# The beginning of a decoder layer's mixer: keys from row pieces, turns of the normalised rows inside the value projection, and query banks emptied ahead of the next weight split

## Chip, cores and metric

The kernel runs on one core of a Trainium2 chip. The metric is device time in microseconds from the start of the program to its end; smaller is better. Engines are named as in the profile: PE is TensorE, PEld its weight loads, DVE is VectorE, ACT is ScalarE, POOL is GpSimd, SP is SyncE, which here only issues DMAs.

## What is computed

One decoder layer over 256 tokens of width 1024, all in fp32. The part that matters here is the beginning of the token mixer:

```
h = layer_norm(x, ln0_g, ln0_b)                     # 256 x 1024
proj = h @ w_in                                     # 256 x 6664
qkv, a, bt, z, xc, gb, gc, qm, gl = split(proj)
qkv = silu(causal_depthwise_conv(qkv, conv_qkv))    # 4 taps, 1536 channels
g = -(exp(a_log) * softplus(a + dt_bias))           # decay of each head
beta = sigmoid(bt)
...                                                 # gated delta rule, short conv
kv = mem @ w_mem_kv                                 # mem 256 x 1024
km, vm = split(kv, 2)                               # 512 key, 512 value columns
...                                                 # attention over mem, gates, w_o
x1 = layer_norm(alpha * h + mixer, ln1_g, ln1_b)
out = layer_norm(alpha * x1 + moe(x1), ln2_g, ln2_b)  # top 4 of 32 experts
```

The experts read all of `w_gate_up` and `w_down`: 32 experts of six 2 MB chunks each.

## The kernel before

**Products.** A 32-bit product in the mixer is made of three faster ones: each operand is split in a `hi` part (type fp32r) and a `lo` part, the rest, and PE adds hi x hi, hi x lo and lo x hi (function `three`, L1171 to L1173). So each weight has to be split before use: ACT casts to `w_hi` (L1048), then DVE or POOL subtracts to `w_lo` (L759). The table `LO_ENGINE` says which of the two does it for a piece.

**Weights.** SP brings mixer weights in slots of 2 MB (8 k-tiles of 128 rows x 512 columns), three raw slots in turn. A slot is split in four pieces of 128 x 1024 values; three split pieces can exist at a time (`SPLITS = 3`), so the split of piece q + 3 (a `prep` step) waits until piece q is used up. Slot 0 holds the key weights, slot 1 the value weights, slots 2 to 4 those of the twelve query, key and value units of the delta rule (`("qkv", 0)` to `("qkv", 11)`, called query units here), and so on to slot 20. Slot 0 comes in four DMAs by columns: each takes 128 of the 512 columns of all 1024 rows, which is 512 bytes in a row of HBM.

**Order.** `mixer_schedule` writes one list of steps, and each engine walks through this list in a loop, taking the steps that concern it. The list begins: turns of `mem` (`memT`, PE transposes into a bank, ACT and DVE split the result), four key units (`km`, each one piece, 24 matmuls of 256 columns), layer norm of the two token tiles (`ln`), the value projection (`vm`: two tiles, 48 matmuls of 512 columns, piece by piece, in `project_rows`), turns of the normalised rows (`hT`), the transposed convolution taps (`cols`), then query units, with the decay's small projection `ab` (24 matmuls of 256 columns against 8 weight columns) after the second of them, its transpose `abT` after the third, and `decay functions` (ACT) after the fourth. Later the steps of the delta rule (`g`) lie between units.

**Banks.** Units that fill a PSUM bank take banks 0 to 2 in turn (`bank_of`), so a unit waits until the unit three before it has been emptied. A query unit is emptied by DVE alone: one multiply for the first tap (L1632) and three multiply-adds (L1635); ACT then applies silu (L1027). A `prep` step stands ahead of the unit whose piece it waits for, so ACT casts and DVE subtracts the next piece before they touch that unit's bank.

**POOL.** Its list of mask constants (`masks`, `decay_masks`) stands ahead of all steps, and `level_masks` after `prep` 8.

**After the mixer.** The experts' chunks go into a ring of 12 slots. SP issues a chunk's DMA as soon as the slot's last content is used; the first three take the mixer's raw slots when the last weight pieces are split, and most of the others wait for the last matmul of `w_o` (L1215).

Of the kernel before, what the change touches and what calls it, by code (L numbers as in the profile page):

```python
# [33 lines left out]
ALU = mybir.AluOpType  # L34
# [3 lines left out]
P = 128  # L38
D = 1024
T = 256  # L40
NT = T // P
KD = D // P
H = 4
# [56 lines left out]
def mixer_schedule():  # L100
# [63 lines left out]
NOT_UNITS = ("decay functions", "g", "prep", "ln", "ya", "sum hi", "sum", "soft", "log decay", "cols", "ab split")  # L164
# [4 lines left out]
def hybrid_layer(nc, x, mem, ln0_g, ln0_b, w_in, conv_qkv, conv_mix, a_log, dt_bias, gdn_norm,  # L169
                 w_mem_kv, w_br, w_o, ln1_g, ln1_b, w_router, b_router, w_gate_up, b_gate_up,  # L170
                 w_down, b_down, ln2_g, ln2_b, out):
    with ExitStack() as ctx:
# [173 lines left out]
        piece_in = [sem(f"piece_in{n}") for n in range(4)]  # L346
# [17 lines left out]
        ab_split, ab_act, ab_dve = sem("ab_split"), sem("ab_act"), sem("ab_dve")  # L364
# [29 lines left out]
        piece_end, joint = {}, 0  # L394
        for u in UNITS:
# [11 lines left out]
        LO_ENGINE[0:12] = ["dve"] * 5 + ["pool"] * 4 + ["dve"] * 3  # L407
# [8 lines left out]
        def piece_views(q):  # L416
# [6 lines left out]
            elif MIXER_SLOTS[n] == ("kv", W) or kind == "wo":  # L423
# [73 lines left out]
        def pe_gdn(pe, name):  # L497
# [20 lines left out]
            elif name == "decay":  # L518

                pe.wait_ge(g_dve, GD["scalars"])  # L520
                for p in range(NPB):
                    mm(out4(p), spread(g_log, p // H, p % H), block_upper[:], start=True, stop=True)
# [239 lines left out]
        def slot_dma(sp, n, j=0):  # L762
# [10 lines left out]
            if n == 0:  # L773
                sp.dma_start(dst[:, :, j * P:(j + 1) * P], src[:, :, j * P:(j + 1) * P]).then_inc(piece_in[j], 16)
            else:
                sp.dma_start(dst, src).then_inc(raw_in[n % RAW], 16)

# [17 lines left out]
        MIXER_FILLS = [len(range(r or RAW, N_MIX, RAW)) if r < RAW else 0 for r in range(RING)]  # L795
# [30 lines left out]
        def _(sp):  # L826
            def bcast(dst, src, done):
                sp.dma_start(dst, src).then_inc(done, 16)

            slot_dma(sp, 0, 0)  # L830
            sp.dma_start(mem_tok, mem[0].rearrange("(t p) d -> p t d", p=P)).then_inc(mem_in, 16)
            for j in range(1, 4):
                slot_dma(sp, 0, j)
            slot_dma(sp, 1)
            sp.dma_start(hx[:], x[0].rearrange("(t p) d -> p t d", p=P)).then_inc(x_in, 16)
            bcast(lnp0[:, 0, :], ln0_g.rearrange("(a d) -> a d", a=1).broadcast_to([P, D]), lnp_in[0])
            bcast(lnp0[:, 1, :], ln0_b.rearrange("(a d) -> a d", a=1).broadcast_to([P, D]), lnp_in[0])
            rows = small_rows
# [80 lines left out]
        def _(pool):  # L919
# [16 lines left out]
            def masks():  # L936
# [3 lines left out]
                for n in range(LEVELS + 1):  # L940
# [950 lines left out]
```

## Time and profile before

| | |
|---|---|
| median of 3 runs | 1269.95 us (1269.81 to 1270.58) |
| the profiled execution: its own time | 1270.24 us |
| its span | 1268.5 us |
| PE busy | 1218.5 us, 96% |
| DVE busy | 400.8 us, 32% |
| ACT busy | 239.2 us, 19% |
| POOL busy | 141.1 us, 11% |
| DMA | 453.45 MB, mean 357 GB/s over the span |

The busy time of PE says little alone: an engine that runs slowly is also busy. The strip in 40 slices (31.7 us each) shows three stages. In the first slice PE is 80% busy and DMA over 90%; in slices 2 to 10 PE is over 90% busy and DMA between 10% and 70%; from slice 12 on both are over 90%, with 424 to 430 GB/s.

### The profile page before, as it was taken

To read this page: it belongs to the slowest core of one execution; us is meant where nothing else is said; L and a number is where in the kernel's file an instruction comes from. 1 tells how busy PE (TensorE), PEld (TensorE's weight loads), DVE (VectorE), ACT (ScalarE), POOL (GpSimd) and SP (SyncE) were. 2 spreads that over 40 slices of the span, in tenths; PEclk is the share of its full clock that TensorE was granted. 3 is DMA by queue.
4 is the path that set the end of the run, shared out by engine and by line. 5 is a ranking of instruction groups with operands and counts; after the bars stand their busy time and mean duration, and the time that the engine had idled before them with its cause. 6 is when DMAs were issued, how large, how long until landed. Compare 5 with 4: busy or idle time off the path is not lost.

```text
span 1268.5 us, 17229 instructions
## 1 busy us (share of the span) xinstructions
PE 1218.5 (96%) x7155; PEld 616.8 (49%) x7155; DVE 400.8 (32%) x787; ACT 239.2 (19%) x385; POOL 141.1 (11%) x105
## 2 busy tenths in 40 slices
PE   8799999999999999999999999999999999999995
PEld 7699999998843333333333333333333333333332
DVE  5685563534521221222222122122122222222114
ACT  4364344444310000010000000000000000000001
POOL 4433422455200000000000000000000000000000
PEclk9899999999999999999999999999999999999998
DMA  9533313595799999999999999999999999999995
GB/s 306 198 134 134 134 68 134 205 360 184 281 399 424 428 427 428 427 428 428 430 428 430 428 427 428 430 428 430 428 427 427 429 427 429 429 426 428 428 427 209
DMA packets 56412, 453.45 MB, mean 357 GB/s; under 512 B 6877, under 2 KB 11050, under 8 KB 31786
## 3 DMA queue, kind: packets, MB, share of 16 engines
q1 hardware_dynamic: 56362, 452.71, 86.3%
q8 instruction: 40, 0.66, 0.2%
q14 instruction: 10, 0.08, 0.0%
HBM read 451.64 MB, written 1.05 MB: 357 GB/s over the span
## 4 chain that ended last, share of the span: by engine, by line
PE 78%; DMA 9%; SPq 4%; DVE 4%; ACT 2%; issue 2%; POOL 0%; another core or an unknown queue 0%; DVEq 0%; ACTq 0%
PE bank L1357 30%; PE bank L1429 15%; DMA late<-in_w_gate_up_dram 8%; PE bank L1171 5%; PE bank L1172 5%; PE bank L1173 5%; PE bank L1328 4%; PE bank L1442 4%; SPq L792 4%; PE bank L1343 2%; PE bank L1417 2%; ACT late L1143 1%; DMA early<-in_ln_b_dram 1%; PE bank L1437 1%; DVE w_lo L759 1%
## 5 line engine op out<-in xcount | busy, mean ns | idle before, releaser
L1357 PE MATMUL bank<-late 128*64 128x512 f32 x1536 | 343.2, 595 | 5.1 <-DMA late<-in_w_gate_up_dram 5.1
L1429 PE MATMUL bank<-late 128*64 128x512 f32 x1024 | 230.1, 602 | 6.2 <-ACT late L1143 6.2
L1357 PEld LDWEIGHTS bank<-late 128*64 128x64 f32 x1536 | 106.7, 137 | 222.7 <-issue 209.8
L1429 PEld LDWEIGHTS bank<-late 128*64 128x64 f32 x1024 | 71.4, 138 | 142.9 <-issue 129.1
L1171 PE MATMUL bank<-act_hi,w_hi 128*128 128x256 f32 x448 | 129.4, 289 | 3.1 <-DVE early L1635 2.5
L1172 PE MATMUL bank<-act_lo,w_hi 128*128 128x256 f32 x448 | 125.8, 281 | 0.0
L1173 PE MATMUL bank<-act_hi,w_lo 128*128 128x256 f32 x448 | 125.8, 281 | 0.0
L1775 DVE TENSOR_SCALAR late<-bank 128x512 f32<-128x512 f32 x32 | 22.1, 692 | 308.2 <-PE bank L1357 308.2
L1357 PE MATMUL bank<-raw,late 128*64 128x512 f32 x512 | 116.7, 598 | 1.2 <-DMA raw<-in_w_gate_up_dram 1.2
L759 POOL TENSOR_TENSOR w_lo<-raw,w_hi 128x1024 fp32r<-128x1024 f32 x33 | 81.2, 2463 | 127.1 <-ACT w_hi L1048 127.1
L1171 PEld LDWEIGHTS bank<-act_hi,w_hi 128*128 128x128 f32 x448 | 84.3, 188 | 5.3 <-DVE early L1635 3.3
L1172 PEld LDWEIGHTS bank<-act_lo,w_hi 128*128 128x128 f32 x448 | 84.5, 189 | 0.1
L1173 PEld LDWEIGHTS bank<-act_hi,w_lo 128*128 128x128 f32 x448 | 84.4, 188 | 0.0
L1786 DVE COPY late<-bank 64x512 f32<-64x512 f32 x32 | 22.2, 694 | 191.3 <-PE bank L1429 191.3
L1136 ACT COPY late<-bank 128x512 f32<-128x512 f32 x33 | 19.3, 586 | 321.9 <-PE bank L1328 321.9
L1048 ACT CAST w_hi<-raw 128x1024 fp32r<-128x1024 f32 x56 | 58.5, 1046 | 90.2 <-issue 59.4
L1357 PEld LDWEIGHTS bank<-raw,late 128*64 128x64 f32 x512 | 34.0, 136 | 72.3 <-issue 69.0
L1442 PE MATMUL bank<-late 64*128 64x512 f32 x256 | 63.6, 615 | 1.0 <-DVE late L1846 1.0
L1145 ACT COPY late<-bank 64x512 f32<-64x512 f32 x32 | 18.5, 579 | 233.3 <-PE bank L1429 233.3
L1328 PE MATMUL bank<-hx,late 128*64 128x512 f32 x264 | 62.3, 592 | 0.0
L1141 ACT ACTIVATE late<-late 128x512 f32<-128x512 f32 x32 | 20.1, 629 | 179.7 <-DVE late L1775 179.7
L1790 DVE COPY late<-bank 128x256 f32<-128x256 f32 x31 | 13.2, 425 | 117.9 <-PE bank L1437 117.9
(319 smaller groups left out, 1194.4 us busy)
## 6 DMA issues: line engine op xcount, KB each, us to landing
late<-in_w_gate_up_dram SPq DMA_DIRECT2D x96, 2048.0 KB, 36.4
late<-in_w_down_dram SPq DMA_DIRECT2D x64, 2048.0 KB, 35.8
raw<-in_w_gate_up_dram SPq DMA_DIRECT2D x32, 2048.0 KB, 34.5
raw<-in_w_in_dram SPq DMA_DIRECT2D x8, 2048.0 KB, 8.7
early<-in_w_in_dram SPq DMA_DIRECT2D x6, 2048.0 KB, 8.4
raw<-in_w_br_dram SPq DMA_DIRECT2D x3, 2048.0 KB, 7.8
raw<-in_w_mem_kv_dram SPq DMA_DIRECT2D x4, 512.0 KB, 7.9
raw<-in_w_mem_kv_dram SPq DMA_DIRECT2D x1, 2048.0 KB, 10.9
```

The costliest lines, as they stand in the source:

```text
L759: ops.tensor_tensor(lo, src, as_f32(hi), ALU.subtract).then_inc(split_lo[who], 1)
L792: sp.dma_start(dst, src).then_inc(landed, 16)
L1048: a.copy(hi, src).then_inc(split_hi, 1)
L1171: mm(o, l_hi, r_hi, start=start, stop=False)
L1172: mm(o, l_hi, r_lo, start=False, stop=False)
L1173: return mm(o, l_lo, r_hi, start=False, stop=stop)
L1328: ins = mm(ps[0][64 * c:64 * c + 64, :], onehot[:, t, :], hx[:, t, 512 * c:512 * (c + 1)], start=(t == 0), stop=(t == NT - 1))
L1343: mm(ps[1 + n][64 * c:64 * c + 64, :], e_row[rows, :], bgu[rows, :], start=True, stop=False)
L1357: ins = mm(bk[64 * c:64 * c + 64, :], x_slotT[:, k % 4, 64 * (k // 4):64 * (k // 4) + 64], w[:, kk, at + 512 * c:at + 512 * (c + 1)], star ...
L1417: ins = tr(ps[3][:, c * P:(c + 1) * P], h_tok[:, c:4 * P:4], ident[:])
L1429: ins = mm(ps[3][64 * c:64 * c + 64, :], hidT[:, kk, 64 * q:64 * q + 64], w[:, kk, c * 512:(c + 1) * 512], start=(q == 0 and kk == 0), sto ...
L1442: ins = mm(ps[4 + 2 * t + c][:, :], scatter[64 * c:64 * c + 64, t * P:(t + 1) * P], y_tok[64 * c:64 * c + 64, :], start=False, stop=True, ...
```

## The change

Everything is in the first part of the mixer, and in the order around query units.

- SP asks for `mem` first, then two pieces of key weights, `x`, the other two, the layer norm's parameters, and then the value weights in four DMAs where there was one. Key and value pieces are cut by rows: two k-tiles of 128 rows, all 512 columns, so 2048 bytes in a row of HBM. The router's weights come after slot 5.
- With row pieces each key piece serves all four key units: `project_keys` keeps four banks (4 to 7) open and adds each piece's 24 matmuls to them. ACT copies all four at once afterwards (`km copy`).
- The turns of the normalised rows leave the banks in rotation; `turn_tile` makes them inside the value projection, before its third piece, in banks 4 to 7.
- The statistics of the layer norm are split from its application. `LO_ENGINE` has new entries for the first pieces.
- For query units the `prep` step now stands behind the unit. ACT does the first tap (a copy with a scale), and DVE the other three. The cast of the small decay weights and most of the decay's elementwise work go from DVE to ACT.
- POOL's mask constants are spread between its pieces.

```diff
...
-    order = [("prep", 0)] + [("memT", n) for n in range(4)] + [("prep", 1), ("prep", 2)]
-    order += [("km", n) for n in range(4)] + [("ln", 0, t) for t in range(NT)] + [("vm", n) for n in range(NT)]
-    order += [("hT", t, j) for j in range(2) for t in range(NT)] + [("prep", 9), ("cols",), ("prep", 10)]
-    order += [("qkv", 0), ("ab split",), ("qkv", 1), ("ab", 0), ("qkv", 2), ("abT", 0), ("qkv", 3), ("decay functions",)]
+    order = [("memT", 0), ("prep", 0), ("memT", 1), ("prep", 1), ("memT", 2), ("memT", 3)]
+    order += [("ln stats", t) for t in range(NT)] + [("prep", 2), ("prep", 3)] + [("ln root", t) for t in range(NT)]
+    order += [("km", 0), ("ln", 0, 0), ("prep", 4), ("prep", 5), ("ln", 0, 1), ("prep", 6), ("km copy",), ("prep", 7), ("prep", 8)]
+    order += [("hT", t, j) for t in range(NT) for j in range(2)] + [("prep", 9), ("vm", 0), ("prep", 10), ("vm", 1), ("cols",)]
+    order += [("ab split",)]
+    order += [("qkv", 0), ("qkv", 1), ("ab", 0), ("qkv", 2), ("abT", 0), ("qkv", 3), ("decay functions",)]
...
-        n = {"km": 1, "qkv": 1, "z": 1, "xc": 1, "gc": 1, "gb": 1, "qm": 1, "gate": 1}.get(s[0], 0)
+        n = {"qkv": 1, "z": 1, "xc": 1, "gc": 1, "gb": 1, "qm": 1, "gate": 1}.get(s[0], 0)
         if s[0] == "br":
             n = s[2] % 2
             uses[s] = [q]
-        if s[0] in ("vm", "wo"):
+        if s[0] in ("km", "vm", "wo"):
             n = 4 * (s[-1] == 0)
         if n:
             uses[s] = list(range(q, q + n))
-            out += [("prep", m + SPLITS) for m in uses[s] if m + SPLITS < 4 * N_MIX and ("prep", m + SPLITS) not in order]
+            preps = [("prep", m + SPLITS) for m in uses[s] if m + SPLITS < 4 * N_MIX and ("prep", m + SPLITS) not in order]
+            out += [s] + preps if s[0] == "qkv" else preps + [s]
             q += n
-        out.append(s)
+        else:
+            out.append(s)
...
+        for q in PIECES_OF["km", 0]:
+            joint += 1
+            piece_end[q] = (joint_piece, joint) if joint < 4 else (km_full, H)
+        joint = 3
...
-        LO_ENGINE[0:12] = ["dve"] * 5 + ["pool"] * 4 + ["dve"] * 3
+        LO_ENGINE[0:12] = ["dve", "pool", "dve", "pool"] + ["dve"] * 3 + ["pool"] * 2 + ["dve", "pool", "dve"]
...
-            if n == 0:
-                sp.dma_start(dst[:, :, j * P:(j + 1) * P], src[:, :, j * P:(j + 1) * P]).then_inc(piece_in[j], 16)
+            if kind == "kv":
+                sp.dma_start(dst[:, 2 * j:2 * j + 2, :], src[:, 2 * j:2 * j + 2, :]).then_inc(piece_in[4 * n + j], 16)
...
+            sp.dma_start(mem_tok, mem[0].rearrange("(t p) d -> p t d", p=P)).then_inc(mem_in, 16)
             slot_dma(sp, 0, 0)
-            sp.dma_start(mem_tok, mem[0].rearrange("(t p) d -> p t d", p=P)).then_inc(mem_in, 16)
-            for j in range(1, 4):
-                slot_dma(sp, 0, j)
-            slot_dma(sp, 1)
+            slot_dma(sp, 0, 1)
             sp.dma_start(hx[:], x[0].rearrange("(t p) d -> p t d", p=P)).then_inc(x_in, 16)
+            slot_dma(sp, 0, 2)
+            slot_dma(sp, 0, 3)
             bcast(lnp0[:, 0, :], ln0_g.rearrange("(a d) -> a d", a=1).broadcast_to([P, D]), lnp_in[0])
             bcast(lnp0[:, 1, :], ln0_b.rearrange("(a d) -> a d", a=1).broadcast_to([P, D]), lnp_in[0])
+            for j in range(4):
+                slot_dma(sp, 1, j)
...
-            sp.dma_start(wr[:], w_router[0].rearrange("(k p) e -> p k e", p=P)).then_inc(router_in, 16)
-            sp.dma_start(br_bc[:], b_router.broadcast_to([P, NE])).then_inc(router_in, 16)
             for n in range(3, N_MIX):
                 slot_dma(sp, n)
+                if n == 5:
+                    sp.dma_start(wr[:], w_router[0].rearrange("(k p) e -> p k e", p=P)).then_inc(router_in, 16)
+                    sp.dma_start(br_bc[:], b_router.broadcast_to([P, NE])).then_inc(router_in, 16)
...
+            before_mask()
+            block_masks(range(0, 4))
+            LEVEL_AFTER = {10: 0, 12: 1, 14: 2, 16: 3, 18: 4, 20: 5}
...
+                    if s[1] == 1:
+                        block_masks(range(4, LEVELS + 1))
+                    if s[1] == 3:
+                        decay_masks()
+                    if s[1] in LEVEL_AFTER:
+                        level_mask_of(LEVEL_AFTER[s[1]])
+                    if s[1] == 22:
+                        chunk_masks()
...
                 elif kind == "hT":
+                    act.wait_ge(h_turned, 2 * t + j + 1)
...
-                elif kind == "ln":
+                elif kind == "ln root":
+                    ln_root_of(0, s[1])
+                elif kind == "ln" and s[1] == 1:
                     ln_root_of(*s[1:])
-                elif kind == "km":
-                    a.copy(kmT[:, s[1], :], bank(s)).then_inc(free, 1)
+                elif kind == "km copy":
+                    for n in range(H):
+                        act.wait_ge(km_full, n + 1)
+                        a.copy(kmT[:, n, :], ps[4 + n][:, 0:T]).then_inc(km_copied, 1)
+                elif kind == "ab split":
+                    act.wait_ge(ab_in, 16)
+                    a.copy(w_ab_hi[:], w_ab).then_inc(ab_hi, 1)
...
                 elif kind == "qkv":
+                    if s[1] == 0:
+                        act.wait_ge(cols_ready, 1)
+                    act.wait_ge(bank_full[bank_of(s)], turn_of(s))
+                    a.activation(qkvT[:, s[1], :], bank(s), ACT.Copy,
+                                 scale=small_cols[:, 36 + s[1]:37 + s[1]]).then_inc(first_tap, 1)
                     if s[1] >= 1:
                         silu(s[1] - 1)
                     if s[1] == 11:
                         silu(11)
                 elif kind == "decay functions":
-                    act.wait_ge(ab_dve, 1)
-                    a.activation(ea, adt[:, 0, :], ACT.Exp)
-                    a.activation(beta, beta, ACT.Exp, scale=-1.0)
-                    step(a.activation(t_b, t_b, ACT.Exp))
-                    a.activation(t_b, t_b, ACT.Ln, bias=1.0).then_inc(ab_act, 2)
+                    act.wait_ge(bank_free[bank_of(("abT", 0))], turn_of(("abT", 0)))
+                    a.activation(t_c, pre_g, ACT.Relu)
+                    step(a.activation(t_b, pre_g, ACT.Abs))
+                    step(a.activation(ea, adt[:, 0, :], ACT.Exp))
+                    a.mul(ea, ea, -1.0)
+                    step(a.activation(beta, beta, ACT.Exp, scale=-1.0))
+                    a.activation(beta, beta, ACT.Identity, bias=1.0)
+                    step(a.activation(t_b, t_b, ACT.Exp, scale=-1.0))
+                    a.activation(t_b, t_b, ACT.Ln, bias=1.0).then_inc(ab_act, 1)
...
+            def project_keys():
+                for j in range(4):
+                    hi, lo = piece(PIECES_OF["km", 0][j])
+                    wait_copied(pe, "memT", j + 1)
+                    for n in range(H):
+                        for kk in range(2):
+                            k = 2 * j + kk
+                            ins = three(ps[4 + n][:, 0:T], hi[:, kk, n * P:(n + 1) * P], lo[:, kk, n * P:(n + 1) * P],
+                                        src_hi[:, k, :], src_lo[:, k, :], k == 0, k == KD - 1)
+                        if j == 3:
+                            ins.then_inc(km_full, 1)
+                    if j < 3:
+                        ins.then_inc(joint_piece, 1)
+            def turn_tile(t):
+                pe.wait_ge(ln_done, t + 1)
+                pe.wait_ge(km_copied, H)
+                for j in range(2):
+                    for k in range(4):
+                        ins = tr(ps[4 + 2 * t + j][:, k * P:(k + 1) * P], hx[:, t, (4 * j + k) * P:(4 * j + k + 1) * P], ident[:])
+                    ins.then_inc(h_turned, 1)
...
+                    if s == ("vm", 0) and j == 2:
+                        turn_tile(t)
...
-                    full()
                     o = qkvT[:, c, :]
-                    step(d.tensor_scalar(o, bk[:, 0:T], small_cols[:, 36 + c:37 + c], None, ALU.mult))
+                    v.wait_ge(first_tap, c + 1)
                     for back in range(1, 4):
...
-                    v.wait_ge(free, turn_of(s))
-                    step(d.tensor_scalar(t_a, pre_g, -1.0, None, ALU.mult))
-                    d.tensor_tensor(t_b, t_a, pre_g, ALU.min).then_inc(ab_dve, 1)
-                    step(d.tensor_scalar(t_c, pre_g, 0.0, None, ALU.max))
...
```

SP at the start of its list, before (`raw` is a weight slot; `early` is an area that holds `mem`, the layer norm's parameters and slot 2; `hx` holds `x`):

```order
L774 DMA raw<-in_w_mem_kv_dram 128x8x128
L831 DMA early<-in_mem_dram 128x2x1024
L774 DMA raw<-in_w_mem_kv_dram 128x8x128 x3
L776 DMA raw<-in_w_mem_kv_dram 128x8x512
L835 DMA hx<-in_x_dram 128x2x1024
L828 DMA early<-in_ln_g_dram 128x1024
L828 DMA early<-in_ln_b_dram 128x1024
L839 DMA small_rows<-in_conv_qkv_dram 48x128
```

and after:

```order
L847 DMA early<-in_mem_dram 128x2x1024
L787 DMA raw<-in_w_mem_kv_dram 128x2x512 x2
L850 DMA hx<-in_x_dram 128x2x1024
L787 DMA raw<-in_w_mem_kv_dram 128x2x512 x2
L845 DMA early<-in_ln_g_dram 128x1024
L845 DMA early<-in_ln_b_dram 128x1024
L787 DMA raw<-in_w_mem_kv_dram 128x2x512 x4
L858 DMA small_rows<-in_conv_qkv_dram 48x128
```

`mem` has moved ahead of the first key piece and `x` between the key pieces; the one value DMA stood ahead of `x` and is now four behind the parameters. A key piece was 128x8x128 and is 128x2x512.

ACT between query units 2 and 4, before (L1048 casts a weight piece, L1027 is silu, L1068 to L1071 are the decay functions):

```order
L1048 CAST w_hi<-raw 128x1024
L1027 ACTIVATE early<-early 128x256
L1048 CAST w_hi<-raw 128x1024
L1027 ACTIVATE early<-early 128x256
L1068 ACT_TABLE_LOAD
L1068 ACTIVATE tiny<-adt 128x4
L1069 ACTIVATE tiny<-tiny 128x8
L1070 ACTIVATE tiny<-tiny 128x8
L1071 ACT_TABLE_LOAD
L1071 ACTIVATE tiny<-tiny 128x8
L1048 CAST w_hi<-raw 128x1024
```

and after (L1071 is the cast of a weight piece, L1096 the first tap, L1050 silu, L1104 to L1111 the decay functions; rows begin one cast earlier):

```order
L1071 CAST w_hi<-raw 128x1024
L1096 ACTIVATE early<-bank,small_cols 128x256
L1050 ACTIVATE early<-early 128x256
L1071 CAST w_hi<-raw 128x1024
L1096 ACTIVATE early<-bank,small_cols 128x256
L1050 ACTIVATE early<-early 128x256
L1071 CAST w_hi<-raw 128x1024
L1104 ACTIVATE tiny<-tiny 128x8
L1105 ACTIVATE tiny<-tiny 128x8
L1106 ACT_TABLE_LOAD
L1106 ACTIVATE tiny<-adt 128x4
L1107 ACTIVATE tiny<-tiny 128x4
```

Each cast stood ahead of its unit's silu and now stands behind the first tap and silu; each query unit has one more ACT instruction, and the decay functions have eight where they had four.

## Rows read from the trace of the kernel before

**Rows 1.** Chain of waits, pieces near the end: start us, us, what.
```profile
1123.41 48.39 DMA late<-in_w_gate_up_dram
...
1181.68 48.84 DMA late<-in_w_gate_up_dram
```
**Rows 2.** Waits of SP's queue, 300 to 360 us: total, times, longest us.
```profile
SPq L792 <- PE bank L1215: 13.7, 1, 13.7
```
**Rows 3.** Stretches: from:to, length, busy PE PEld DVE ACT POOL, PEclk, DMA, GB/s.
```profile
404.00:1240.00 836.00, 821.60 (x3916) 280.57 (x3914) 188.68 (x400) 70.80 (x119) 0.00 (x0) 1.00 1.01 428
...
0.00:24.66 24.66, 21.10 (x142) 20.22 (x143) 10.50 (x12) 12.24 (x18) 13.82 (x30) 0.93 0.98 332
...
31.00:41.74 10.74, 6.63 (x31) 5.26 (x30) 5.91 (x5) 4.16 (x7) 9.62 (x12) 0.84 0.98 342
41.74:59.17 17.43, 13.29 (x97) 11.38 (x96) 11.60 (x17) 6.28 (x7) 5.55 (x8) 0.90 0.44 153
59.17:72.54 13.37, 12.11 (x100) 11.68 (x99) 10.81 (x21) 9.60 (x15) 2.90 (x2) 1.00 0.06 11
13.00:22.00 9.00, 9.00 (x77) 8.91 (x77) 4.32 (x5) 4.34 (x7) 0.96 (x1) 1.00 1.04 398
```
**Rows 4.** Stretches of 1 us, the same columns.
```profile
8.00:9.00 1.00, 1.00 (x7) 1.00 (x6) 0.05 (x1) 0.59 (x1) 0.82 (x3) 0.50 1.20 291
15.00:16.00 1.00, 1.00 (x11) 1.00 (x10) 0.92 (x1) 0.32 (x2) 0.00 (x0) 1.00 1.06 391
```
**Rows 5.** PE in order of time: start us, us, instruction, idle before.
```profile
7.44 3.42 PE L1244 MATMUL bank<-ident,early 128*128 128x128 f32 x16 [2.14 <-DMA early<-in_mem_dram]
...
22.44 0.40 PE L1171 MATMUL bank<-w_hi,src_hi 128*128 128x512 f32 x1
22.68 0.39 PE L1172 MATMUL bank<-w_lo,src_hi 128*128 128x512 f32 x1
...
34.48 0.50 PE L1171 MATMUL bank<-w_hi,src_hi 128*128 128x512 f32 x1 [3.48 <-POOL w_lo L759]
...
36.32 0.63 PE L1173 MATMUL bank<-w_hi,src_lo 128*128 128x512 f32 x1
36.74 0.63 PE L1171 MATMUL bank<-w_hi,src_hi 128*128 128x512 f32 x1
...
51.91 0.28 PE L1171 MATMUL bank<-act_hi,w_ab_hi 128*8 128x256 f32 x1 [4.14 <-DVE w_ab_lo L1566]
...
63.63 0.38 PE L1171 MATMUL bank<-act_hi,w_hi 128*128 128x256 f32 x1 [1.13 <-DVE early L1635]
...
95.26 0.39 PE L1171 MATMUL bank<-act_hi,w_hi 128*128 128x256 f32 x1 [1.41 <-DVE early L1635]
```
**Rows 6.** DVE in order of time.
```profile
24.66 0.16 DVE L1516 RECIPROCAL tiny<-tiny 128x1 f32<-128x1 f32 x1 [1.04 <-DMA early<-in_ln_b_dram]
24.86 2.43 DVE L1521 SCALAR_TENSOR_TENSOR hx<-hx,tiny,early 128x1024 f32<-128x1024 f32 x1
27.33 1.28 DVE L1523 SCALAR_TENSOR_TENSOR hx<-hx,tiny,early 128x1024 f32<-128x1024 f32 x1
...
49.28 2.15 DVE L1565 CAST w_ab_hi<-early 128x64 fp32r<-128x64 f32 x1
...
52.19 1.51 DVE L1635 SCALAR_TENSOR_TENSOR early<-bank,small_cols,early 128x255 f32<-128x255 f32 x3
...
60.41 1.23 DVE L759 TENSOR_TENSOR w_lo<-raw,w_hi 128x1024 fp32r<-128x1024 f32 x1 [3.54 <-ACT w_hi L1048]
```
**Rows 7.** POOL in order of time.
```profile
49.04 2.34 POOL L759 TENSOR_TENSOR w_lo<-raw,w_hi 128x1024 fp32r<-128x1024 f32 x1 [3.84 <-ACT w_hi L1048]
```
**Rows 8.** ACT in order of time.
```profile
59.33 1.05 ACT L1048 CAST w_hi<-raw 128x1024 fp32r<-128x1024 f32 x1 [8.71 <-issue]
...
66.84 1.28 ACT L1071 ACT_TABLE_LOAD   x1
68.13 0.21 ACT L1071 ACTIVATE tiny<-tiny 128x8 f32<-128x8 f32 x1
...
110.05 0.39 ACT L1073 ACTIVATE early<-bank 128x256 f32<-128x256 f32 x1
```

More of the change, by code:

```diff
@@ L163 @@
 SCHEDULE, PIECES_OF = mixer_schedule()
-NOT_UNITS = ("decay functions", "g", "prep", "ln", "ya", "sum hi", "sum", "soft", "log decay", "cols", "ab split")
+NOT_UNITS = ("decay functions", "g", "prep", "ln", "ya", "sum hi", "sum", "soft", "log decay", "cols", "ab split",
+             "km", "km copy", "hT", "ln stats", "ln root")
 UNITS = [s for s in SCHEDULE if s[0] not in NOT_UNITS]
@@ L345, in hybrid_layer @@
         router_in, ebias_in = sem("router_in"), sem("ebias_in")
-        piece_in = [sem(f"piece_in{n}") for n in range(4)]
+        piece_in = [sem(f"piece_in{n}") for n in range(8)]
+        km_full, km_copied = sem("km_full"), sem("km_copied")
+        h_turned, h_split = sem("h_turned"), sem("h_split")
+        ab_hi, first_tap = sem("ab_hi"), sem("first_tap")
         raw_in = [sem(f"raw_in{n}") for n in range(RAW)]
@@ L794, in hybrid_layer @@
         RING_IN = raw_in + first_in + late_in + [spare_in, once_in]
-        MIXER_FILLS = [len(range(r or RAW, N_MIX, RAW)) if r < RAW else 0 for r in range(RING)]
+        MIXER_FILLS = [len(range(first_fill(r), N_MIX, RAW)) if r < RAW else 0 for r in range(RING)]
         def ring_place(m, rounds=0):
@@ L934, in _, with before_mask, block_masks @@
             eng.memset(upad[:, :, 0:2], 0.0).then_inc(pads, 1)
-            def masks():
+            def before_mask():
                 eng.affine_select(out=before[:], in_=ones[:], pattern=[[1, P]], compare_op=ALU.is_gt,
                                   fill=0.0, base=0, channel_multiplier=-1)
-                for n in range(LEVELS + 1):
+            def block_masks(levels):
+                for n in levels:
                     s = 1 << n
@@ L1038, in _ @@
                     n = q // 4
-                    if n == 0:
+                    if n < 2:
                         act.wait_ge(piece_in[q], 16)
                     else:
-                        act.wait_ge(raw_in[n % RAW], 16 * len(range(n % RAW or RAW, n + 1, RAW)))
+                        act.wait_ge(raw_in[n % RAW], 16 * len(range(first_fill(n % RAW), n + 1, RAW)))
                     if q >= SPLITS:
@@ L1255, in _ @@
                         keep_warm(10, ps[7])
-                    pe.wait_ge(ln_done, t + 1 if kind == "hT" else NT + t + 1)
+                    pe.wait_ge(ln_done, NT + t + 1)
                     for k in range(4):
@@ L1549, in _ @@
                     continue
+                if kind == "ln stats":
+                    t = s[1]
+                    if t == 0:
+                        v.wait_ge(x_in, 16)
+                    step(half_stats(t, 0))
+                    step(half_stats(t, 1))
+                    variance(t)
+                    continue
                 if kind == "ln":
@@ L1604, in _ @@
                     continue
-                if kind == "sum hi":
+                if kind in ("sum hi", "km", "km copy", "ln root"):
+                    continue
+                if kind == "hT":
+                    hi_parts += 1
+                    t, j = s[1:]
+                    v.wait_ge(bank_hi, hi_parts)
+                    hi, lo = (p[:, 4 * j:4 * j + 4, t * P:(t + 1) * P] for p in (act_hi, act_lo))
+                    d.tensor_tensor(lo, ps[4 + 2 * t + j][:, :].rearrange("p (a b) -> p a b", b=P), as_f32(hi),
+                                    ALU.subtract).then_inc(h_split, 1)
                     continue
```

72 lines of the change are left out of this document (25 added, 47 removed).

## Prediction

> **What bounds the kernel now.** Begin at the end. The chain of waits, read near its end, shows two pieces of 48 us each in which only the landing of expert weights is waited for [rows 1]. The stretch 404 to 1240 us has DMA at 1.01 of its time and 428 GB/s with PE at 0.98 [rows 3]: the expert stage is as long as the stream of its weights takes, and it can shrink only if the stream starts earlier. SP's waits tell when it starts: it stood 13.7 us before the last matmul of the output projection (L1215) [rows 2]. So the start of the stream is tied to the progress of the mixer, whose time is on PE, and whatever PE gains ahead of it should reach the end of the kernel one to one.
>
> Now the mixer's first 73 us, in order of time, as PE sees them. Full speed is seen at 13 to 22 us: 77 key matmuls of 256 columns in 9.00 us at a granted clock of 1.00 (2.4 GHz), 0.117 us each [rows 3]. A value matmul of 512 columns takes 0.235 us (22.44 to 22.68); at the clock's half level (1.2 GHz) it takes 0.42 (36.32 to 36.74) [rows 5]. PE waits 2.14 us for `mem`, then turns it in 3.42 us at half clock; waits 3.48 us for a value piece from POOL at 34.48; waits 4.14 us for the decay weights at 51.91; waits 1.13 us for the taps at 63.63, and 1.41 us at 95.26 [rows 5]. Stretches give the same: of 10.74 us up to 41.74, where the first query unit starts, PE is busy 6.63 at clock 0.84; of the 17.43 us to 59.17 it is busy 13.29 at clock 0.90; of the next 13.37 us it is busy 12.11 [rows 3].
>
> **Part 1: up to the first query unit (41.74 us before).** I rebuild PE's time line.
>
> Arrival. While the column pieces are moved (512 bytes in a row), DMA brings 291 GB/s; with long rows 391 [rows 4]. The key slot is 2.10 MB: 7.2 us at the one rate, 5.4 at the other, 1.8 us saved for everything behind it. Of what is needed before the values (mem 1.05, keys 2.10, values 2.10, x 1.05, parameters 1.05: 7.35 MB), the last landed at 24.66 [rows 6], when 332 x 24.66 = 8.2 MB had moved [rows 3], so a transfer lands when up to 0.9 MB behind it have moved too. After, the last value piece lands at about 24.7 - 1.8 = 22.9, and the parameters, now ahead of the 2.10 MB of values, 5.4 us earlier, 17.5. `mem` loses the 0.52 MB piece ahead of it: 7.44 - 1.6 = 5.8. Key pieces then follow at 7.2, 8.6, and, behind x (11.8), 13.3 and 14.8 (1.35 us for 0.52 MB, 2.7 for x).
>
> *The Trainium skill, "DMA: Bandwidth & Descriptors", Specifications, puts the line rate at transfers of 512 bytes and more; by that rule the row pieces bring nothing, and the 1.8 us fall away. The trace disagrees with it here: 291 against 391 GB/s.*
>
> Keys. Turn and split of `mem`, cast of the first piece by ACT (1.05 [rows 8]) from 7.3, behind it the subtraction on DVE (1.23 [rows 6]) behind one of a bank: first key matmul at 9.8 (before: 10.55). A piece is 24 matmuls, 2.8 us. The third piece is late: cast at 14.4, but DVE has the statistics of x till 15.1 and subtracts till 16.4, while PE is through with the second at 15.4: a new wait of 1.0 us. The fourth (POOL, 2.34 [rows 7]) is ready at 18.3, in time. Keys end at 9.8 + 4 x 2.8 + 1.0 = 22.0.
>
> Values. Their first piece is cast at 20.4, behind the normalisation of the first tile on DVE (17.5 to 20.6 with 1.28 us an instruction, 1.1 more where it runs into POOL, as 2.43 shows [rows 6]): subtracted at 21.9 to 22.9. The last one lands at 22.9, is cast at 26.0, as a split place comes free, and is ready from POOL at 28.4, when PE needs it at 32.8. So the wait of 3.48 us goes, and the half clock behind it. Values take 48 x 0.235 = 11.3, the turns inside them 16 x 0.11 = 1.7 (3.42 us for 16 at half clock [rows 5]); with 0.6 for the first piece, the end is 22.0 + 11.3 + 1.7 + 0.6 = 35.6. The turns' split (ACT and DVE) lies beside the last value pieces. Gain: 41.74 - 35.6 = 6.1 us.
>
> **Part 2: query units 0 to 2 with `ab` (41.74 to 59.17).** The work is 4 x 24 matmuls = 96 x 0.117 = 11.2, and 0.2 for small ones. Before, DVE cast the decay weights at 49.28 in 2.15 us [rows 6], beside a subtraction on POOL [rows 7], behind the taps of unit 0. After, ACT casts them ahead of unit 0, in some 0.2 us, and `ab` comes only at 35.6 + 5.6 = 41.2. Wait 4.14 and the half clock after it go. Gain: 17.43 - 11.4 = 6.0 us.
>
> **Part 3: units 3 to 6 and the decay functions (59.17 to 72.54).** Time runs from E, the end of unit 2. ACT, for a unit: cast 1.05, first tap and silu 0.39 each [rows 8], 1.83 of 2.8 us: it keeps pace, until eight decay instructions (0.2 each, and the waits between them) and three table loads of 1.28 come. They start at E + 4.9, behind the cast of piece 14; first tap of unit 4 at E + 9.4, table, silu, cast of piece 15 at E + 12.1, DVE done at E + 13.4. PE needs that piece at E + 11.5. Wait: about 1.9 us, against 1.26 idle before [rows 3]. The unit's bank, free 2.0 us after its end (first tap 0.39, taps 1.51 [rows 6]) instead of 4 or more, takes the wait of 63.63 away; this new one, for a piece, takes its place. Cost: 0.7 us. Nothing else stands behind ACT there but first taps, whose banks PE needs no earlier than the piece.
>
> **Costed at nothing.** POOL's masks: it has 5.6 us for a piece of 2.34, a level adds under 1. The four key copies on ACT (0.39 each) lie beside the first values. `x`, the parameters, the small rows have landed before they are used; if not, the wait is that of the first value piece, in the range. The router's weights are used 280 us later. From unit 12 on the order is as before. At 95.26 the wait for the taps becomes one for the next piece, by the same exps on ACT: no change.
>
> **Sum.** 6.1 + 6.0 - 0.7 = 11.4 us. Against the profiled execution's 1270.24 us (its span 1268.5 and 1.7 around it): 1258.8. The median is 0.3 under that execution, so the forecast is 1258.6.
>
> Bounds. What the trace doesn't show is the start of the keys and the first tap on ACT. If `mem` lands as before and keys start at 10.55, and the first value piece has DVE's contention in full, 2 us go: 9.4. If PE's idle time ahead of the keys (1.9 us of it after the last turn) drops the clock, as 2.14 us did before, the first 24 matmuls cost 2.3 us more, less the 1.0 that they would wait anyway.
>
> **Rivals.**
>
> *A, the start gives part of it back.* Half clock on the keys (+1.3), and pieces that land 2.2 us later than reckoned, since they queue behind x: 3.5 us, 1262.1. For it: the 2.14 us of idle and the 0.50 clock after it [rows 4, 5]. Against: a later piece partly takes the place of waits I have counted.
>
> *B, 512 bytes are enough.* The DMA rate rises by nothing, all lands 1.8 us later, PE follows: 1260.4. *(That is the DMA page's rule of the Trainium skill, named above.)* Against: rows 4.
>
> *C, more goes.* Banks freed 2.5 us earlier also end the waits at 63.63 and 95.26 without a new one for a piece (1.13 + 1.41 + the 0.7 not paid): 3.2 us more, 1255.4. For it: both waits name the taps. Against: ACT's table loads lie ahead of the next cast.
>
> *D, nothing.* The stream's rate or start is set by something other than the mixer, the gain is swallowed: 1270. Against: rows 2.
>
> *E, slower.* ACT becomes the bound of all query units: the first tap read from a bank with a scale from a column, behind it silu, then the cast, all in one strict row. PE's time for a unit is 2.8 us; ACT's is 1.83. From 3.8 us a unit on, twelve units eat the 11.4 us; at 4.0, which would take a first tap of 2.5 us, they cost 12 x 1.2 = 14.4, and the time is 1258.6 + 14.4 = 1273.0. Against: 0.39 for such an instruction from a bank [rows 8].
>
> *The Trainium skill, "SBUF — State Buffer", speaks of one port pair that DVE and GpSimd lock against each other for a whole instruction; by it the cast's 2.15 us [rows 6] are waiting for POOL, and ACT is free of that; but by it the new POOL pieces beside the normalisation would cost up to 2.3 us each. That is in A.*
>
> **How the numbers follow.** Forecast 0.56, A 0.20, B 0.03, C 0.13, D 0.04, E 0.04. The forecast's own range is 1257 to 1260.6. The range for all reaches to C and past A: 1255.3 to 1263.2. What can be told from no change here is 0.2%, 2.5 us: faster has all but D and E, 0.92; same 0.04; slower 0.04.
>
> **What would show it.** First key matmul near 9.8 us at full clock, the first query unit near 35.6, no wait ahead of `ab`, one of 2 us for a piece four units later, in the stretch after it nothing new; 428 GB/s in the expert stage and the same length from the last L1215 to the end. Wrong would be: a first query unit after 39, half clock in keys or values, waits for the first tap (ACT) in most query units, or a mixer that ends 11 us earlier with a kernel that doesn't.

## The result, and the profile after

| | before | changed |
|---|---|---|
| median | 1269.88 us (1269.34 to 1270.58, 4 runs) | 1262.27 us (1260.65 to 1262.91, 4 runs) |
| the profiled execution: its own time | 1270.24 us | 1260.65 us |
| its span | 1268.5 us | 1258.9 us |

The ratio is 0.9939 (95% interval 0.9927 to 0.9951): 7.6 us faster, where 11.4 were forecast. The forecast was 1258.6, its own range 1257 to 1260.6, the range over all rivals 1255.3 to 1263.2; the median lies outside the first and inside the second. In a later set the changed kernel took 1262.91 us (1261.44 to 1263.68, 5 runs), ratio 0.9944 (0.993 to 0.9957).

The expert stage and its start, in the changed kernel: a stretch, with the columns of [rows 3], and SP's wait.

```profile
404.00:1230.00 826.00, 811.22 (x3864) 276.78 (x3859) 185.97 (x393) 69.70 (x117) 0.00 (x0) 1.00 1.01 428
```
```profile
SPq L809 <- PE bank L1279: 12.9, 1, 12.9
```

As in [rows 2, 3]: 428 GB/s, and SP still waits for `w_o`. The mixer shows how much arrives. Take the turns of the delta rule's output (the step `onorm`, eight PE transposes), far behind the change: their first weight load is at 233.9 us before and at 225.6 after, 8.3 us earlier; the span is 9.6 shorter. These turns serve below as a mark of how far a trace has come.

PE in order of time, as [rows 5]:

```profile
6.03 1.59 PE L1310 MATMUL bank<-ident,early 128*128 128x128 f32 x12
8.15 0.66 PE L1310 MATMUL bank<-ident,early 128*128 128x128 f32 x4 [0.53 <-DVE src_lo L1693]
9.81 0.38 PE L1211 MATMUL bank<-src_hi,w_hi 128*128 128x256 f32 x1 [1.01 <-DVE w_lo L772]
...
15.98 0.39 PE L1211 MATMUL bank<-src_hi,w_hi 128*128 128x256 f32 x1 [0.22 <-DVE w_lo L772]
...
34.98 0.36 PE L1211 MATMUL bank<-act_hi,w_hi 128*128 128x256 f32 x1
...
46.41 0.29 PE L1333 MATMUL bank<-ident,early 8*128 8x8 f32 x2
...
59.85 0.36 PE L1211 MATMUL bank<-act_hi,w_hi 128*128 128x256 f32 x1 [1.60 <-DVE w_lo L772]
...
83.15 0.36 PE L1211 MATMUL bank<-act_hi,w_hi 128*128 128x256 f32 x1 [1.57 <-DVE w_lo L772]
...
89.56 0.36 PE L1211 MATMUL bank<-act_hi,w_hi 128*128 128x256 f32 x1 [3.33 <-POOL w_lo L772]
```

The first key matmul is at 9.81, the first query unit at 34.98 (41.74 before), unit 2 ends at 46.41 (59.17), unit 7 starts at 59.85 (72.54), and what started at 95.26 starts at 83.15. Up to there the gain is 12.1 us. Then PE waits 3.33 us for a weight piece (piece 22) from POOL. Before, there was no wait at that place.

ACT, POOL and DVE around that wait, in the changed kernel (L1050 silu, L1071 the cast of a weight piece, L1708 the product of squares, L772 the subtraction):

```profile
81.65 0.46 ACT L1096 ACTIVATE early<-bank,small_cols 128x256 f32<-128x256 f32 x1
82.02 0.40 ACT L1050 ACTIVATE early<-early 128x256 f32<-128x256 f32 x1
84.47 0.42 ACT L1050 ACTIVATE early<-early 128x256 f32<-128x256 f32 x1 [2.04 <-DVE early L1701]
84.79 1.98 ACT L1071 CAST w_hi<-early 128x1024 fp32r<-128x1024 f32 x2
```
```profile
85.98 3.44 POOL L772 TENSOR_TENSOR w_lo<-early,w_hi 128x1024 fp32r<-128x1024 f32 x1 [11.44 <-ACT w_hi L1071]
```
```profile
84.92 2.29 DVE L1708 TENSOR_TENSOR early<-early 128x2048 f32<-128x2048 f32 x1 [0.49 <-ACT early L1050]
87.13 3.37 DVE L772 TENSOR_TENSOR w_lo<-early,w_hi 128x1024 fp32r<-128x1024 f32 x1
```

Unit 11 is the last query unit, and its step has two silus: that of unit 10 and its own. Its own must wait for DVE's taps of the same unit, so ACT stands idle for 2.04 us; and the cast of piece 22, behind it in the reordered list, starts at 84.79, 2.4 us after the silu of unit 10. POOL's subtraction then overlaps the product of squares and takes 3.44 us where 2.4 is usual.

### The profile page after: what moved, and what is told of

It reads as the page before. It is cut to its first block, busy times and chain, and to the rows that moved or that the text cites. A ratio compares the mean times of both kernels' runs of the same rounds, so it can differ in the third digit from the quotient of the medians.

```text
span 1258.9 us, 17233 instructions
## 1 busy us (share of the span) xinstructions
PE 1211.7 (96%) x7155; PEld 612.6 (49%) x7155; DVE 391.5 (31%) x768; ACT 243.9 (19%) x402; POOL 147.0 (12%) x106
## 4 chain that ended last, share of the span: by engine, by line
PE 80%; DMA 8%; DVE 4%; ACT 3%; SPq 2%; issue 1%; POOL 1%; another core or an unknown queue 0%; DVEq 0%; ACTq 0%; POOLq 0%
PE bank L1421 31%; PE bank L1493 16%; DMA late<-in_w_gate_up_dram 8%; PE bank L1211 6%; PE bank L1212 5%; PE bank L1213 5%; PE bank L1506 4%; PE bank L1392 4%; PE bank L1407 2%; SPq L809 2%; PE bank L1481 2%; ACT late L1183 1%; ACT w_hi L1071 1%; PE bank L1501 1%; DMA raw<-in_w_mem_kv_dram 0%
## 5 line engine op out<-in xcount | busy, mean ns | idle before, releaser
L772 POOL TENSOR_TENSOR w_lo<-raw,w_hi 128x1024 fp32r<-128x1024 f32 x33 | 81.0, 2456 | 109.0 <-ACT w_hi L1071 108.9
L1071 ACT CAST w_hi<-raw 128x1024 fp32r<-128x1024 f32 x56 | 58.6, 1047 | 79.8 <-issue 46.2
## 6 DMA issues: line engine op xcount, KB each, us to landing
raw<-in_w_gate_up_dram SPq DMA_DIRECT2D x32, 2048.0 KB, 34.9
```

What stands on the lines that cost most here:

```text
L772: ops.tensor_tensor(lo, src, as_f32(hi), ALU.subtract).then_inc(split_lo[who], 1)
L1071: a.copy(hi, src).then_inc(split_hi, 1)
```

## Experiments

Each is the changed kernel with one edit, if nothing else is said; `...` marks code left out. The kernel before, on the same chips, took 1270.0 to 1270.3 us.

**The last silu behind the cast.**

```diff
                     a.copy(hi, src).then_inc(split_hi, 1)
+                    if q == 22:
+                        silu(11)
...
-                    if s[1] == 11:
-                        silu(11)
```

> The changed kernel, with only the last silu (of query unit 11) moved behind the cast of weight piece 22. In its trace PE waits 3.33 us at 89.56 us for that piece: ACT stood 2.04 us for the taps of unit 11 and did the last silu before it cast the piece. Theory T (the order on ACT makes this wait): the cast comes 2.4 us earlier, the wait shrinks to under 1 us, and the time falls by 2.4 to 3.3 us against the changed kernel's 1262.3, to about 1259.4. Rival P (POOL's subtraction is late because DVE's product of squares holds it up, 3.44 us for 2.4): the wait stays above 2 us and the time within 1 us of 1262.3.

Measured 1256.82 us, ratio to the kernel before 0.9891 (0.9876 to 0.9907). The wait is gone from PE. ACT's cast, POOL's subtraction and DVE's squares, in this kernel:

```profile
82.01 1.03 ACT L1071 CAST w_hi<-early 128x1024 fp32r<-128x1024 f32 x1
84.15 0.42 ACT L1050 ACTIVATE early<-early 128x256 f32<-128x256 f32 x1 [1.11 <-DVE early L1701]
```
```profile
83.19 2.41 POOL L772 TENSOR_TENSOR w_lo<-early,w_hi 128x1024 fp32r<-128x1024 f32 x1 [8.96 <-ACT w_hi L1071]
```
```profile
84.60 3.15 DVE L1708 TENSOR_TENSOR early<-early 128x2048 f32<-128x2048 f32 x1 [0.48 <-ACT early L1050]
```

The subtraction starts 2.8 us earlier, ahead of the squares, and takes 2.41 us; now the squares, which begin while it runs, are the stretched ones, with 3.15 us for 2.29, and nobody waits for them. So theory T stands, and P has a part: of the 3.8 us by which the piece is ready earlier 1.0 is contention. In the medians this one line is worth 5.5 to 6 us, more than T's 2.4 to 3.3. The traces bear out most of it: the `onorm` turns come at 221.7, against 225.6 and 227.0 in two traces of the changed kernel, so 3.9 and 5.3 us earlier. The gap between those two is a fall of the clock behind the wait (see "Constants in the wait").

**No reorder at all.**

```diff
-            out += [s] + preps if s[0] == "qkv" else preps + [s]
+            out += preps + [s]
```

> The changed kernel with the prep steps of query units ahead of the unit again, on all engines, the rest as changed (first tap on ACT stays). Theory T (the reorder costs more than it gives): the wait of 3.33 us for piece 22 goes, those of 1.60 and 1.57 us for pieces 15 and 21 turn into waits for banks of about the same length; 1262.3 - 3.3 = 1259.0. Rival R (the reorder pays, by banks that come free 2.5 us earlier): waits for banks appear in query units, 3 us or more in sum, and the time is 1262 or above.

Measured 1256.08 us, 0.9884 (0.9869 to 0.9899), and again, in another set:

> The changed kernel without the reorder of query units, again, for the two runs beside it. Both theories: 1256.1, within 1.5 us.

Measured 1255.95 us, 0.9892 (0.9877 to 0.9907). This beats the changed kernel by 6 to 7 us; the intervals do not meet. PE's waits for pieces 15 and 22 are gone, one of 0.63 us for taps has come at 50.50, and what is left of that at 83.15 is a wait for taps:

```profile
81.92 0.38 PE L1211 MATMUL bank<-act_hi,w_hi 128*128 128x256 f32 x1 [0.81 <-DVE early L1701]
```

Banks that come free earlier gave nothing that the pieces, coming later, didn't take back.

**Every silu behind the cast, the first tap ahead of it.**

```diff
+                    if 12 <= q <= 22:
+                        silu(q - 12)
+                    if q == 22:
+                        silu(11)
...
-                    if s[1] >= 1:
-                        silu(s[1] - 1)
-                    if s[1] == 11:
-                        silu(11)
```

> The changed kernel with every silu of a query unit behind the cast of the next weight piece; the first tap stays ahead of it. So a bank is emptied early and the piece is not behind a silu and its table load. Theory T: the waits of 1.60 (59.85 us), 1.57 (83.15) and 3.33 (89.56) all shrink by the table load and silus ahead of the cast (1.7 to 2.4 us each), about 5.5 us in sum: 1262.3 - 5.5 = 1256.8. Rival P (DVE and POOL are late, not ACT): under 2 us, 1260.5 or more.

Measured 1257.15 us, 0.9892 (0.9877 to 0.9907). T's number holds. The three waits are 0.36, 0.33 and 0.75 us, but new ones have come, of 1.10 us for `log decay` on DVE and of 0.57 us for a piece. It is no better than no reorder.

**The reorder alone, in the kernel before.**

```diff
-            out += [("prep", m + SPLITS) for m in uses[s] if ...]
+            preps = [("prep", m + SPLITS) for m in uses[s] if ...]
+            out += [s] + preps if s[0] == "qkv" else preps + [s]
...
-        out.append(s)
+        else:
+            out.append(s)
```

> The kernel before with only the reorder of query units (prep steps behind the unit); its beginning, its first tap on DVE and its small decay work are untouched. Theory T (reorder is a loss at the last query unit, a small gain earlier): the wait of 1.13 us at 63.63 goes or turns, a wait of about 3 us for piece 22 appears: 1269.9 + 1 to 3 = 1272. Rival R (reorder is part of the gain): 1268.5 or less.

Measured 1270.21 us, ratio 1.0002 (0.9993 to 1.0011): nothing. Neither theory's number, though T's wait for piece 22 came. PE in this kernel:

```profile
49.88 0.28 PE L1173 MATMUL bank<-act_hi,w_ab_hi 128*8 128x256 f32 x1 [1.91 <-DVE w_ab_lo L1568]
...
90.44 0.36 PE L1173 MATMUL bank<-act_hi,w_hi 128*128 128x256 f32 x1 [1.38 <-DVE w_lo L761]
97.36 0.55 PE L1173 MATMUL bank<-act_hi,w_hi 128*128 128x256 f32 x1 [3.85 <-POOL w_lo L761]
```

It wins at the decay weights (1.91 for 4.14 [rows 5]) and at 63.63 (1.13, now none), and loses it behind the last query unit, 3.85 us. Behind that wait the granted clock is 0.50 from 97 to 102 us, and the `onorm` turns are 1.6 us later than before (235.5 for 233.9); the medians do not show it. In the changed kernel the loss is left and the wins are not: without the reorder it has no wait at the decay weights either, and of the waits up to 60 us it has 0.63 us for taps, where with the reorder it has 1.60 us for piece 15.

**Constants in the wait.** First the changed kernel itself once more, unedited:

> The changed kernel itself, to have it on the same chip as the runs beside it. Both theories: 1262.3, within its spread of 1260.6 to 1263.

Its time is in the section on the result. Its trace differs from the first mainly at one place; the stretches around the long wait, of the first trace and of this one:

```profile
85.00:90.00 5.00, 1.67 (x14) 1.50 (x13) 5.00 (x2) 3.27 (x5) 4.02 (x2) 1.00 0.00 2
90.00:95.00 5.00, 5.00 (x46) 5.00 (x45) 1.70 (x2) 2.26 (x3) 4.20 (x5) 1.00 0.69 220
```
```profile
85.00:90.00 5.00, 1.68 (x14) 1.50 (x14) 5.00 (x2) 3.21 (x5) 4.08 (x2) 1.00 0.01 2
90.00:95.00 5.00, 5.00 (x32) 5.00 (x32) 0.44 (x1) 0.82 (x1) 4.15 (x5) 0.66 0.70 246
```

The same work, the same wait, but a granted clock of 0.66 of full behind it, and 32 matmuls where the other had 46. The turns of `onorm` come at 227.0 instead of 225.6. The full clock of the first trace is the exception: of six traces with a wait of 3.3 to 3.9 us for piece 22, five have half clock behind it. Besides this one they are `keys_in_512_bytes` (0.75 at 90 to 95 us, 0.91 at 95 to 100), `values_ahead_of_x` (0.75 at 100 to 105), `reorder_alone` (above) and `small_weights_on_dve`:

```profile
90.00:95.00 5.00, 4.12 (x19) 4.16 (x20) 1.81 (x1) 0.00 (x0) 4.73 (x6) 0.50 0.41 129
```

In the traces without the wait the clock is 1.00 there. So PE was given matmuls on constants to do in the wait (`z`, 2 is the unit that uses piece 22):

```diff
+                    if s == ("z", 2):
+                        keep_warm(14, ps[b])
```

> The changed kernel with 14 matmuls of 128 columns on constants put into the wait ahead of the unit that uses weight piece 22 (their result is overwritten by the unit). They take about 3 us, so PE is not idle there. Theory K (the long wait costs more than its 3.33 us, because in some executions the clock falls to its half level behind it: 90.0 to 93.4 us in one of the two traces of this kernel): the clock stays full there, the median falls by 0.5 to 1.5 us against 1262.6 and the spread narrows. Rival: the 5.5 us that the moved silu won are the order's own, and the time here is as before, 1262.6 or a little more.

Measured 1261.57 us, 0.9932 (0.9919 to 0.9946), range 1260.7 to 1262.41. That is 1.3 us below the run of the changed kernel in the other set and 0.7 below its first, but the intervals overlap. The clock stays full in this trace, and the unit behind the wait starts at 89.83 (89.56 in the changed kernel's first trace):

```profile
85.00:90.00 5.00, 4.87 (x43) 4.68 (x42) 4.74 (x2) 3.61 (x6) 3.68 (x2) 1.00 0.01 2
90.00:95.00 5.00, 5.00 (x45) 5.00 (x45) 1.76 (x2) 1.97 (x3) 4.55 (x5) 1.00 0.61 189
```

That the clock falls behind this wait in most traces is shown. What it costs in the median is not: 0.7 to 1.3 us is of the size of the 1.4 us between the two traces, but within the noise. The wait of 3.33 us and this 1.4 make 4.7 of the 5.5 to 6 us that the moved silu is worth; the rest is not located.

**Keys in rows of 512 bytes.**

```diff
-                sp.dma_start(dst[:, 2 * j:2 * j + 2, :], src[:, 2 * j:2 * j + 2, :]).then_inc(piece_in[4 * n + j], 16)
+                for b in range(4 if n == 0 else 1):
+                    cols = slice(b * P, (b + 1) * P) if n == 0 else slice(0, W)
+                    sp.dma_start(dst[:, 2 * j:2 * j + 2, cols], src[:, 2 * j:2 * j + 2, cols]).then_inc(piece_in[4 * n + j], 16)
...
-                        act.wait_ge(piece_in[q], 16)
+                        act.wait_ge(piece_in[q], 64 if n == 0 else 16)
```

> The changed kernel with the four key pieces fetched in 512-byte rows (four DMAs of 128 columns for each piece, same order, same bytes). Theory T (short rows cost bandwidth: 291 against 391 GB/s): everything behind the keys lands 1.8 us later, the first query unit starts 0.5 to 1.8 us later, the time rises by as much. Rival B (512 bytes are enough): the rate in the first 10 us stays where it is and the time is the same.

Measured 1264.46 us, 0.9957 (0.9942 to 0.9972). Its interval overlaps that of the changed kernel, but no run of it (1264.14 to 1264.91) is as fast as the slowest of the changed kernel (1263.68). A stretch of this kernel, and the same of the changed one:

```profile
8.00:13.00 5.00, 3.54 (x28) 3.31 (x28) 3.76 (x6) 3.30 (x5) 2.39 (x2) 1.00 1.03 343
```
```profile
8.00:13.00 5.00, 3.85 (x31) 3.61 (x32) 4.44 (x7) 3.17 (x6) 2.85 (x3) 1.00 1.04 404
```

The rate is lower while the keys' rows are short, the third key piece is cast at 14.42 instead of 12.66, and the first query unit starts at 36.5 instead of 34.9 (both against the changed kernel's second trace; 12.73 and 34.98 in the first). Rival B falls: what the Trainium skill, "DMA: Bandwidth & Descriptors", Specifications, says of 512 bytes doesn't hold for these loads. The time rises by 1.6 us against the changed kernel of the same set and by 2.2 against the first; T gave 0.5 to 1.8. (SP issues 12 DMAs more here, and each is smaller. The DMA engines are busy all through the stretch, 1.03, and in the kernel before the short rows came in DMAs of 512 KB and moved at 291 GB/s [rows 4], so I take the row length for the cause; the number of DMAs was not varied by itself.)

**Values ahead of x and the parameters.** The loop over `slot_dma(sp, 1, j)` and, behind it, the DMA of `x` stand behind the last key piece.

> The changed kernel with the four value DMAs ahead of x and the parameters, as the kernel before had them. Theory T (the order of the DMAs carries the start): x lands 5.4 us plus the keys' 2.7 later, at about 19 us instead of 11; the statistics stand ahead of the third key piece on DVE, so the keys stall about 7 us, and the first query unit starts about 6 us later: 1268. Rival: the keys alone (row pieces) carry it, 1263 to 1264.

Measured 1271.19 us, 1.0009 (1.0 to 1.0018): the whole gain is gone. PE and DVE:

```profile
24.10 0.58 PE L1211 MATMUL bank<-src_hi,w_hi 128*128 128x256 f32 x1 [8.08 <-DVE w_lo L772]
```
```profile
19.77 1.42 DVE L1570 BATCH_NORM_STATS2 tiny<-hx 128x6 f32<-128x512 f32 x2 [7.76 <-DMA hx<-in_x_dram]
...
22.88 1.17 DVE L772 TENSOR_TENSOR w_lo<-raw,w_hi 128x1024 fp32r<-128x1024 f32 x1
```

DVE takes its list in order: it waits 7.76 us for `x`, and the third key piece, which ACT cast at 11.05, is behind its statistics. T's mechanism, but dearer than T had it: the first query unit starts at 44.33, 9.4 us later where T had 6, and the time is 3.2 us above T's 1268. The stall is 8.08 us for T's 7, and behind it the granted clock is 0.83 over 24.1 to 34 us, which by its two levels is 3.4 us at the half one, an estimated 1.7 us lost.

**The decay's small weights on DVE.** `ab split` behind query unit 0 again, the cast on DVE.

```diff
-                    act.wait_ge(ab_in, 16)
-                    a.copy(w_ab_hi[:], w_ab).then_inc(ab_hi, 1)
+                    pass
...
+                    v.wait_ge(ab_in, 16)
+                    d.tensor_copy(w_ab_hi[:], w_ab).then_inc(ab_hi, 1)
```

> The changed kernel with the cast of the decay's small weights back on DVE, behind the taps of query unit 0, as before. Theory T (the wait of 4.14 us at 51.91 was this cast held up on DVE by POOL): a wait of 1 to 3 us ahead of the small projection comes back, with the half clock behind it 0 to 1.7 more: 1264 to 1266. Rival: the wait had gone with the new order of the pieces anyway, under 0.5 us.

Measured 1263.86 us, 0.9949 (0.9934 to 0.9964). PE waits 0.99 us ahead of `ab`, and the cast takes 0.18 us, not 2.15 [rows 6]: POOL has nothing at that moment (its subtraction begins at 44.33, the cast at 41.40). The time is 1.0 us above the changed kernel of the same set, but the intervals overlap. So the move is worth the wait of 1 us. Wait and time stand at T's lower edge (1 us, 1264), but T's cause, a cast held up by POOL, is absent. It is absent in `reorder_alone` too: there DVE's cast takes 0.19 us and the wait is 1.91, so 2.2 of the 4.14 go with the order of the pieces alone.

**Turns behind the values**, on the kernel with no reorder: both `turn_tile` calls stand behind `project_rows`.

> Without the reorder, and with the turns of the normalised rows behind the value projection instead of inside it (still in banks 4 to 7). Theory T (the turns inside hide the split of their result): PE waits for ACT and DVE to split the last turned tile ahead of query unit 0, 1.5 to 3 us more, so 1258 to 1259. Rival: the split is hidden anyway, within 0.5 us of the run beside it.

Measured 1257.4 us, 0.9903 (0.9888 to 0.9918), against 1255.95. PE waits 1.31 us up to 36.47 for the last tile's split, and the first query unit starts there, where it starts at 34.65 and 35.13 in the two traces with no reorder. In the median it is 1.45, under T's 1.5 to 3; the intervals overlap, the trace has it.

**The first tap on DVE**, on the kernel with no reorder: ACT's `activation` of query units taken out, DVE's `tensor_scalar` put back.

> Without the reorder, and with the first tap on DVE again, as before. It leaves the new beginning and the small decay work on ACT alone. Theory T (the beginning carries the whole gain, the first tap at most 1 us of it by banks freed earlier): 1256 to 1257.5. Rival C of the prediction (banks freed earlier carry 3 us): 1259 or more.

Measured 1257.87 us, 0.9906 (0.9891 to 0.9921), with a range from 1254.51 to 1258.51. PE's two waits for taps are 1.15 and 1.42 us here and 0.62 and 0.82 with the first tap on ACT: 1.1 us. The median is 1.9 us above that of the kernel with no reorder, between T's 1257.5 and rival C's 1259; the range is too wide to see 1.1 us in it.

Not tried alone: row pieces with four open key banks against the old key units, the new entries of `LO_ENGINE`, POOL's constants between its pieces, the decay's elementwise work on ACT, and the later place of the router's weights.

## Why the prediction was right, and where it was not

**What bounds the kernel: right.** The stream is as fast as it was and its start moved with the mixer. From the `onorm` turns to the end of the span it is 1034.6 us before, and 1033.3 and 1033.6 in the two traces of the changed kernel; over all kernels here it is 1031.6 to 1035.7. That scatter, 4 us from the shortest to the longest, is not explained.

**Part 1: right.** Forecast and found: first key matmul 9.8 and 9.81; wait for the third piece 1.0 and 0.22; last value piece's wait gone; first query unit 35.6 and 34.98. The clock is full throughout, so rival A's condition didn't come. One step of the working slipped: the landings of `x` and the last two key pieces (11.8, 13.3, 14.8) are more than the rates beside them give (11.3, 12.7, 14.0), and ACT began to cast the two pieces at 12.73 and 14.08. It cost nothing, since DVE's statistics kept the third piece until 14.8. In the changed list the order of the DMAs is what carries the start (8 us of wait without); what it would give the old list, where the statistics stood behind the keys, was not tried. Short rows would cost 1.6 to 2.2, the turns' old place about 1.5.

**Part 2: the number right (6.0 us gained, as forecast; with Part 1 it is 12.8 by the end of unit 2, for 12.1), the reason half.** The trace's row named DVE's cast; taking it off DVE is worth only 1 us in the new order, and 2.2 of the 4.14 us go with the reorder alone. The contention moved on: in the changed kernel DVE's subtraction of these weights takes 1.83 us beside POOL, where PE's work on units 0 and 1 covers it.

**Part 3: right.** The wait of 1.9 us for piece 15 is 1.60, and PE goes on at E + 13.4, as reckoned (E is 46.41). The stretch is 13.44 us for 13.37 before, so the cost is 0.1 and not 0.7. Rival C's time of 1255.4 was nearly met, at 1255.95 and 1256.08, but by taking the reorder out.

**The step that failed** is, among what was costed at nothing: "From unit 12 on the order is as before. At 95.26 the wait for the taps becomes one for the next piece, by the same exps on ACT: no change." The first wait did turn so (1.41 before, 1.57 after). But unit 11 has two silus, and the second waits for the taps of its own unit. I had walked the reordered row for units 3 to 7 and not for the last one, whose step is different. That put a wait of 3.33 us where none was, and in most traces half clock behind it; moving that one silu takes 5.5 to 6 us off the time. With it, the changed kernel's 1256.8 would have been 1.8 us under the forecast.

**What was luck.** The median, 1262.27, is almost rival A's 1262.1, but A's half clock on the keys and its late pieces are not in the trace. The wide range held the result because it had been drawn for A; the loss that did come was in no rival.

## What to carry to other kernels

When a step is moved behind another in a list that an engine walks in order, walk the first, a middle and the last turn of the loop: the last often holds an extra instruction with a wait of its own, and what is now behind it pays. A DMA order is part of the instruction order: a transfer that an engine waits for early in its list holds up everything behind, landed or not. And a change of several parts should be timed without each: here one part, worth nothing alone, cost nearly half of what the others won (6 to 7 us of 14). Last, price a wait on PE with what the clock may do behind it, not by its length alone.

## What the runs showed of the hardware that I had not expected

The same kernel, with the same wait of 3.3 us on PE, kept its full clock behind it in one profiled execution (46 matmuls in the 5 us behind) and had a granted clock of 0.66 there in another (32 matmuls): with 2.4 and 1.2 GHz as the levels, 3.4 of the 5 us at the lower one. The turns of `onorm` came 1.4 us later in that execution. Over all kernels here with a wait of 3.3 to 3.9 us at that place, five traces of six have the lower level behind it. One trace without a fall says little about the next.

Of POOL's subtraction and DVE's product of squares, the one that began second was stretched, whichever it was. In the changed kernel POOL began at 85.98 with the squares running until 87.21, 1.2 us of overlap, and took 1.0 us more (3.44 for 2.41). With the last silu behind the cast the squares began at 84.60 with POOL running until 85.60, 1.0 us of overlap, and took 0.9 us more (3.15 for 2.29). DVE's own subtraction, shown behind the squares above, began at 87.13 with POOL running until 89.42, and took 3.37 us for 1.23. The clearest case is the decay weights' small subtraction, in the changed kernel, with the POOL piece it ran into:

```profile
36.32 2.40 POOL L772 TENSOR_TENSOR w_lo<-early,w_hi 128x1024 fp32r<-128x1024 f32 x1 [4.19 <-ACT w_hi L1071]
36.97 1.83 DVE L1632 TENSOR_TENSOR w_ab_lo<-early,w_ab_hi 128x64 fp32r<-128x64 f32 x1 [1.51 <-ACT w_ab_hi L1089]
```

It takes 0.22 us with POOL idle (`small_weights_on_dve`); here it ends at 38.80, just behind POOL's 38.72. The Trainium skill, "SBUF — State Buffer", SBUF: two separate sides, says that a GpSimd operation that reads SBUF and a VectorE operation with two inputs in SBUF take their shared ports by an exclusive lock, and the second waits until the first is done. The traces agree: the stretch is about the overlap. In the profile such a wait is no idle time but a longer instruction.
